# Depthwise convolution of a two-block transformer kernel: 12 of 31 taps as 128x32 weights on TensorE over copies shifted through DRAM, 19 taps on VectorE

## Chip, cores and metric

One core of one Trainium2 chip. The time is the device time of one execution in microseconds, the lower the better. Engines are named as in the profile: PE is TensorE, DVE VectorE, ACT ScalarE, POOL GpSimd, SP SyncE; SP issues almost all DMAs, on one queue.

## Reference

512 tokens, width 1024, fp32. Two blocks follow each other. The first is a mixer (gated linear attention and windowed attention) and an MLP. The second has two layers, `x = x + rms_norm(mixer(rms_norm(x)), post_norm)`: layer 0 mixes with attention and pooling, layer 1 with a gated convolution, which is where most of the change lies:

```python
def odd_mixer(h, w_in, dw_w, dw_b, ln_g, ln_b, w_out):
    proj = h @ w_in                                  # 1024 -> 3072
    a, b, gate = jnp.split(proj, [CONV_WIDTH, 2 * CONV_WIDTH], axis=-1)
    glu = a * jax.nn.sigmoid(b)
    conv = lax.conv_general_dilated(                 # each channel by itself, 31 taps, causal
        glu, dw_w.astype(glu.dtype), window_strides=(1,), padding=[(CONV_K - 1, 0)],
        dimension_numbers=('NWC', 'WIO', 'NWC'), feature_group_count=CONV_WIDTH)
    cf = conv.astype(jnp.float32) + dw_b.astype(jnp.float32)
    mu = jnp.mean(cf, axis=-1, keepdims=True)
    var = jnp.mean(jnp.square(cf - mu), axis=-1, keepdims=True)
    cn = (cf - mu) * lax.rsqrt(var + EPS) * ln_g.astype(jnp.float32) + ln_b.astype(jnp.float32)
    y = jax.nn.silu(cn).astype(h.dtype) * jax.nn.silu(gate)
    return y @ w_out
```

## The kernel before

Everything is written by hand in one program per engine, with semaphores between them; no scheduler moves anything.

**Projections.** Every fp32 weight is split into a high half (ACT, `hi`, L1362) and a low half (DVE, `lo`, L1768); activations are split the same way (`hi_turned` L1403 on ACT, `lo_turned` L1812 on DVE). A product of 128x128 by 128x512 is three matmuls, hi by hi, lo by hi, hi by lo (`mm3`, L702 to L704). A *tile* is one 128x512 result: 8 slices of the contraction by 3, 24 matmuls. Weights come in *chunks* of 512 columns, 2 MB each, loaded by SP (`load_chunk`, L639) in two pieces of four slices into one of two slots, when PE has finished the chunk that was in it two chunks ago. A chunk of the convolution's input projection is four DMAs, since it holds 256 columns of `a` and 256 of `b`; all others are two.

**Convolution stage.** In four chunks (N_AB to N_AB+3) PE makes channel tiles, channels on the partitions and tokens in the row, in pairs: a tile of `b`, to which ACT applies the sigmoid, and a tile of `a` ("gated"), from which DVE makes `glu` of channel tile t = 0 to 7, with 30 zero columns ahead of the tokens. Then come four token tiles of each of the two gate chunks, N_G0 and N_G1, then the output projection, chunks N_CO0 and N_CO1. The 31 taps of channel tile t are spread: 4 are matmuls on PE with diagonal 128x128 weights that ACT builds (`diagonal`, L1628; `conv_taps`, L861, in the middle of the next tile of `b`), 16 are multiply-adds on DVE in two chains in PSUM (`tap`, L2113), 11 are products on ACT (L1644) that POOL adds up (L1291, L1295). DVE adds the sums to `ct` (`conv_sum`, L2123), PE turns it to tokens (`turn_conv`, L850), ACT copies it out (`conv_out`, L1650), and after the last the layernorm follows on DVE (statistics L2129, centred L2161, scaled L2171, product with the gate L2179), PE turning each block of 128 tokens (`turn_block`, L840) for the output projection. The order of DVE and ACT in this stage stands in tables (`hooks`), that of PE in `after`.

**Passages.** Between a projection's last chunk and the next stage stand four blocks of 128 tokens (`boundary_blocks`, s = 0, 1, 2): the square sum of the second half (L1376), the post scale, the new residual on DVE (`rt`, L1795), the pre scale (L1391), `normed` on DVE (`un`, L1804), the turn on PE (L840), the halves of the turned block. Into this both engines fit the weight halves of the following chunk: ACT `hi(following, b - 1)` in blocks 1 and 2, DVE `lo(following, b - 2)` in blocks 2 and 3.

Of the kernel before, what the change touches and what calls it, by code (L numbers as in the profile page):

```python
# [5 lines left out]
F32 = mybir.dt.float32  # L6
# [35 lines left out]
PE_TAPS = 4  # L42
DVE_TAPS = 16
ACT_TAPS = TAPS - DVE_TAPS - PE_TAPS
PRODUCTS = ACT_TAPS + 1
COPY_AT = ACT_TAPS - 2

# [21 lines left out]
def all_tiles():  # L69
# [16 lines left out]
    for n in range(N_AB, N_G0):  # L86
        tiles += [(n, m, m, "AD"[m % 2]) for m in range(4)]
# [21 lines left out]
def chunk_dmas(n):  # L109
    return 2 if N_AB <= n < N_G0 else 1  # L110
# [9 lines left out]

def tap_chain(t, m):

    if m >= DVE_TAPS - 2:
        return 0
    return m % 2 if t < 2 else 1 - m % 2

def tap_order(t):

    return (max(m for m in range(DVE_TAPS) if tap_chain(t, m) == 1) + 1,)

# [24 lines left out]
def shape_constants():  # L157
# [10 lines left out]
                           np.broadcast_to(cnt, (P, 64))], axis=1).astype(np.float32)  # L168
# [41 lines left out]
def block_kernel(nc, a, out):  # L210
    ctx = ExitStack()
    with ctx:
# [22 lines left out]
        act_lo = sb("act_lo", [P, KT, TOK], F32R)  # L235
        R = sb("R", [P, TOK])
# [91 lines left out]
        pacc = at("pacc", [P, 2, TOK], arena + 32 * KB)  # L328
# [7 lines left out]
        diag = at("diag", [P, 2, PE_TAPS, P], arena + 52 * KB)  # L336
# [3 lines left out]
        sg = cC("sg", [P, 2, TOK])  # L340
        prod = cC("prod", [P, 4, TOK])
        ct = cC("ct", [P, 2, TOK])
        taps = cC("taps", [P, KT, TAPS])
        tap_rows = at("tap_rows", [TAPS, D], arena + 84 * KB)
# [17 lines left out]
        def vacc(t, which):  # L362

            return (psT[:, 0, :], psT[:, 1, :], ps6[:, :])[(2 * t + which) % 3]

        relF_dram = nc.dram_tensor("relF_dram", [8, REPEAT, 512], F32, kind="Internal").ap()
# [235 lines left out]
        def _(sp):  # L602
# [96 lines left out]
        def _(pe):  # L699
# [465 lines left out]
            pe.wait_ge(taps_in, 16)  # L1165
            pe.wait_ge(ob_done, 4)
            for k in range(KT):
                last = pe.transpose(ps6[:, k * TAPS:(k + 1) * TAPS], tap_rows[:, k * P:(k + 1) * P],
                                    ident[0:TAPS, 0:TAPS])
            last.then_inc(taps_ps, 1)  # L1170
# [3 lines left out]
            after = {(1, 0): 0, (1, 3): 1, (2, 2): 2, (3, 0): 3, (3, 2): 4}  # L1174
            for i in range(4):
                for m in range(4):
                    channel_tile(N_AB + i, m, 0)
                    if m % 2 == 0 and 2 * i + m // 2 >= 1:
                        conv_taps(2 * i + m // 2 - 1)
                    channel_tile(N_AB + i, m, 1)  # L1180
                    if (i, m) in after:
                        turn_conv(after[i, m])
            after = {(0, 1): 5, (1, 0): 6, (1, 2): 7}
            for i in range(2):
                for b in range(NBLK):
                    token_tile(N_G0 + i, b, 0)
                    if i == 0 and b == 0:
# [18 lines left out]
        def _(pool):  # L1206
# [74 lines left out]
            for slot in range(4):  # L1281
                pool.memset(glu[:, slot, 0:CPAD], 0.0).then_inc(pad_set, 1)
            for t in range(KT):
                for m in range(1, ACT_TAPS + 1):
                    made = PRODUCTS * t + m + 1
                    pool.wait_ge(prod_done, made)
                    g = made - 1
                    if m == 1:
                        if t >= 2:
                            pool.wait_ge(conv_done, t - 1)  # L1290
                        pool.tensor_tensor(pacc[:, t % 2, :], prod[:, (g - 1) % 4, :], prod[:, g % 4, :], ALU.add)\  # L1291
                            .then_inc(padd_done, 1)
                    else:
                        pool.wait_ge(padd_done, ACT_TAPS * t + m - 1)
# [934 lines left out]
```

## Time and profile before

| | |
|---|---|
| median of 3 runs | 1126.48 us (1124.2 to 1126.49) |
| the profiled execution | 1125.93 us, span 1124.1 us |
| mean granted clock of PE | 0.96 |
| PE | 1033.6 us busy, 92% |
| DVE, ACT, POOL | 584.4, 468.5, 170.0 us busy |
| DMA | 93.91 MB, mean 84 GB/s |

In a timeline row, the bracket is the time that the engine stood idle before it and what released it; in a group's row, the idle time stands after the bar.

### The profile page before, as it was taken

To read this page: it belongs to the slowest core of one execution; us is meant where nothing else is said; L and a number is where in the kernel's file an instruction comes from. 1 tells how busy PE (TensorE), PEld (TensorE's weight loads), DVE (VectorE), ACT (ScalarE), POOL (GpSimd) and SP (SyncE) were. 2 spreads that over 40 slices of the span, in tenths; PEclk is the share of its full clock that TensorE was granted. 3 is DMA by queue.
4 is the path that set the end of the run, shared out by engine and by line. 5 is a ranking of instruction groups with operands and counts; after the bars stand their busy time and mean duration, and the time that the engine had idled before them with its cause. 6 is when DMAs were issued, how large, how long until landed. Compare 5 with 4: busy or idle time off the path is not lost.

```text
span 1124.1 us, 12285 instructions
## 1 busy us (share of the span) xinstructions
PE 1033.6 (92%) x4847; PEld 824.7 (73%) x4847; DVE 584.4 (52%) x768; ACT 468.5 (42%) x765; POOL 170.0 (15%) x131
## 2 busy tenths in 40 slices
PE   3899999997999999999999979989898899979897
PEld 2677677886788888888888868767677667657676
DVE  5436665235744234333344463366556397777853
ACT  3325562135533334134123354234355557556541
POOL 2200101000000000000000000022000189886300
PEclk8999999998999999999999999989999799999989
DMA  6532102034221252233224214302033222210301
GB/s 213 73 122 76 38 1 76 1 113 150 76 76 75 75 187 75 75 109 116 76 75 149 76 38 132 141 1 75 2 136 120 68 76 76 75 54 27 145 1 75
DMA packets 55823, 93.91 MB, mean 84 GB/s; under 512 B 2581, under 2 KB 23958, under 8 KB 55638
## 3 DMA queue, kind: packets, MB, share of 16 engines
q1 hardware_dynamic: 53648, 90.61, 23.3%
q10 hardware_dynamic: 2118, 2.52, 1.6%
q8 instruction: 39, 0.64, 0.2%
q14 instruction: 18, 0.15, 0.0%
HBM read 90.76 MB, written 2.36 MB: 83 GB/s over the span
## 4 chain that ended last, share of the span: by engine, by line
PE 55%; DVE 8%; ACT 4%; issue 3%; POOL 1%; DMA 1%; SPq 0%; DVEq 0%; POOLq 0%; ACTq 0%
PE acc L702 17%; PE acc L703 17%; PE acc L704 16%; DVE wlr L1768 2%; ACT wh L1362 2%; DVE psT L2113 1%; POOL pacc L1295 1%; PE psT L861 1%; DMA wl<-in_c_w_in_dram 1%; PE ps L861 1%; PE ps L993 1%; DVE rt L1795 1%; DVE act_lo L1812 1%; ACT junk L1391 1%; PE psT L978 1%
## 5 line engine op out<-in xcount | busy, mean ns | idle before, releaser
L1768 DVE TENSOR_TENSOR wlr<-wl,wh 128x2048 fp32r<-128x2048 f32 (+1 forms) x66 | 149.9, 2276 | 96.4 <-ACT wh L1362 96.4
L702 PE MATMUL acc<-act_hi,wh 128*128 128x512 f32 x464 | 187.9, 405 | 1.7 <-DVE act_lo L1812 1.4
L704 PE MATMUL acc<-act_hi,wlr 128*128 128x512 f32 x464 | 182.3, 393 | 0.0
L703 PE MATMUL acc<-act_lo,wh 128*128 128x512 f32 x464 | 182.1, 392 | 0.0
L1362 ACT ACTIVATE wh<-wl 128x2048 fp32r<-128x2048 f32 (+1 forms) x66 | 123.7, 1880 | 61.2 <-DMA wl<-in_w_up_dram 35.1
L702 PE MATMUL acc<-wh,act_hi 128*128 128x512 f32 x320 | 131.3, 410 | 19.0 <-DVE act_lo L1738 7.6
L703 PE MATMUL acc<-wlr,act_hi 128*128 128x512 f32 x320 | 127.6, 399 | 0.0
L704 PE MATMUL acc<-wh,act_lo 128*128 128x512 f32 x320 | 127.6, 399 | 0.0
L1295 POOL TENSOR_TENSOR pacc<-pacc,prod 128x512 f32<-128x512 f32 x80 | 117.5, 1469 | 28.6 <-ACT prod L1644 16.1
L702 PEld LDWEIGHTS acc<-act_hi,wh 128*128 128x128 f32 x464 | 88.4, 191 | 21.7 <-DVE act_lo L1812 1.8
L703 PEld LDWEIGHTS acc<-act_lo,wh 128*128 128x128 f32 x464 | 88.3, 190 | 19.1 <-issue 1.7
L704 PEld LDWEIGHTS acc<-act_hi,wlr 128*128 128x128 f32 x464 | 87.9, 190 | 19.0
L703 PE MATMUL acc<-wlr,hid_hi 128*128 128x512 f32 x256 | 100.8, 394 | 0.0
L702 PE MATMUL acc<-wh,hid_hi 128*128 128x512 f32 x256 | 100.5, 393 | 0.0
L704 PE MATMUL acc<-wh,hid_lo 128*128 128x512 f32 x256 | 99.4, 388 | 0.0
L702 PEld LDWEIGHTS acc<-wh,act_hi 128*128 128x128 f32 x320 | 61.9, 194 | 34.9 <-DVE act_lo L1738 9.3
L702 PE MATMUL acc<-act_hi,w_hi 128*128 128x512 f32 x152 | 65.5, 431 | 10.8 <-DVE act_lo L1730 7.4
L1276 POOL MEMSET uu<- 128x64 f32 x1 | 0.2, 157 | 475.5 <-PE acc L704 475.5
L703 PEld LDWEIGHTS acc<-wlr,act_hi 128*128 128x128 f32 x320 | 62.3, 195 | 13.0 <-issue 0.7
L704 PEld LDWEIGHTS acc<-wh,act_lo 128*128 128x128 f32 x320 | 61.9, 193 | 13.5
L1644 ACT ACTIVATE prod<-glu,taps 128x512 f32<-128x512 f32 x88 | 60.0, 716 | 13.7 <-POOL pacc L1295 13.0
L2113 DVE SCALAR_TENSOR_TENSOR psT<-glu,taps,psT 128x512 f32<-128x512 f32 x83 | 59.7, 750 | 4.7 <-PE psT L861 4.4
(221 smaller groups left out, 1536.8 us busy)
## 6 DMA issues: line engine op xcount, KB each, us to landing
wl<-in_w_up_dram SPq DMA_DIRECT2D x16, 1024.0 KB, 6.3
wl<-in_w_down_dram SPq DMA_DIRECT2D x16, 1024.0 KB, 6.3
raw<-in_w_in_dram SPq DMA_DIRECT2D x18, 512.0 KB, 4.8
wl<-in_a_w_in_dram SPq DMA_DIRECT2D x8, 1024.0 KB, 6.2
wl<-in_c_w_in_dram SPq DMA_DIRECT2D x16, 512.0 KB, 6.2
wl<-in_w_out_dram SPq DMA_DIRECT2D x4, 1024.0 KB, 6.2
wl<-in_ab_w_out_dram SPq DMA_DIRECT2D x4, 1024.0 KB, 7.4
wl<-in_c_w_in_dram SPq DMA_DIRECT2D x4, 1024.0 KB, 6.4
```

Source lines behind the costliest of these rows:

```text
L702: pe.matmul(dst, hi, x_hi, start=first, stop=False)
L703: pe.matmul(dst, hi, x_lo, start=False, stop=False)
L704: return pe.matmul(dst, lo, x_hi, start=False, stop=last)
L861: last = pe.matmul(vacc(t, 0), diag[:, t % 2, m, :], glu[:, t % 4, j:j + TOK], start=m == 0, stop=m == PE_TAPS - 1)
L978: last = pe.transpose(psTf[:, (2 * b + j) * P:(2 * b + j + 1) * P], LG[layer][:, i % 2, j, 1 + b * P:1 + (b + 1) * P], ident[:, :])
L993: last = pe.matmul(ps6[:, 64 * j:64 * j + 64], PT[layer][:, (2 * b + j) * P:(2 * b + j + 1) * P], VTOK[layer][:, kb, 64 * g:64 * g + 64], ...
L1295: pool.tensor_tensor(pacc[:, t % 2, :], pacc[:, t % 2, :], prod[:, g % 4, :], ALU.add)\
L1362: act.activation(wh[slot][:, kk, cols], wl[slot][:, kk, cols], ACT.Copy).then_inc(whi_done, 1)
L1391: act.activation(junk[:, :], rt[:, b, :], ACT.Square, accum_out=ssq[:, s, 16 + b:17 + b])\
L1644: act.activation(prod[:, g % 4, :], glu[:, t % 4, j:j + TOK], ACT.Copy, scale=taps[:, t, j:j + 1])\
L1768: dve.tensor_tensor(wlr[slot][:, kk, cols], wl[slot][:, kk, cols], wh[slot][:, kk, cols].bitcast(F32), ALU.subtract).then_inc(wlo_done, 1)
L2113: ins = dve.scalar_tensor_tensor(out=sums, in0=src, scalar=taps[:, t, m:m + 1], in1=sums, op0=ALU.mult, op1=ALU.add)
```

## The change

`PE_TAPS` goes from 4 to 12, `ACT_TAPS` to none, DVE has 19 (`Y_TAPS` 10, `X_TAPS` 9).

- **Taps on PE.** SP writes `glu` of channel tile t to DRAM (`glu_dram`, L689) and reads it back four times, 32 channels and all four channel groups at a time, each read one token further (`shifted`, L692). Partitions 32j to 32j+31 then hold the groups of 32 channels shifted by j tokens. For each group of 32 channels (c) three matmuls with 128x32 weights (`tapw`, made by POOL from the taps and a pattern of small identities) sum four taps each, 12 in all, at column position 32c of the array (L884).
- **Taps on DVE.** Ten into a sum in SBUF (`ysum`), nine onto PE's sum in PSUM (`xsum`), those of t between those of t - 1; `conv_sum` adds the two.
- **ACT and POOL** have no part in the sums. POOL makes the low halves of N_CO0.
- **Order.** `conv_taps(t)` stands in the middle of the next gated tile (for tile 7, of the second gate tile), `turn_conv(t)` stands later too; the last turn comes after the last gate tile. The weight halves at passages come one block sooner. In the layernorm block 0 is scaled before block 1 is centred.

```diff
+            def shift(t):
+
+                sp.wait_ge(evD_done, evacs_before(TILE_AT[N_AB, 0], "D") + t + 1)
+                if t >= 2:
+                    sp.wait_ge(petap_done, t - 1)
+                sp.dma_start(glu_dram[t], glu[:, t % 4, :]).then_inc(glu_out, 16)
+                sp.wait_ge(glu_out, 16 * (t + 1))
+                for j in range(4):
+                    sp.dma_start(shifted[32 * j:32 * j + 32, t % 2, :, :],
+                                 bass.AP(glu_dram.tensor, t * P * GLUW + j, [[GLUW, 32], [32 * GLUW, 4], [1, SHIFTED]]))\
+                      .then_inc(shift_in[t % 2], 16)
...
             def conv_taps(t):
 
-                pe.wait_ge(evD_done, evacs_before(TILE_AT[N_AB, 0], "D") + t + 1)
-                pe.wait_ge(diag_done, PE_TAPS * (t + 1))
-                if t >= 2:
-                    pe.wait_ge(conv_done, t - 1)
-                for m in range(PE_TAPS):
-                    j = TAPS - PE_TAPS + m
-                    last = pe.matmul(vacc(t, 0), diag[:, t % 2, m, :], glu[:, t % 4, j:j + TOK],
-                                     start=m == 0, stop=m == PE_TAPS - 1)
+                pe.wait_ge(shift_in[t % 2], 4 * 16 * (t // 2 + 1))
+                pe.wait_ge(tapw_done, t + 1)
+                if t >= 3:
+                    pe.wait_ge(conv_done, t - 2)
+                for m in range(PASSES):
+                    for c in range(4):
+                        last = pe.matmul(xsum(t)[32 * c:32 * c + 32, :], tapw[:, t % 2, 4 * m + c, :],
+                                         shifted[:, t % 2, c, 4 * m:4 * m + TOK], start=m == 0, stop=m == PASSES - 1)
...
-            after = {(1, 0): 0, (1, 3): 1, (2, 2): 2, (3, 0): 3, (3, 2): 4}
+            after = {(1, 2): 0, (2, 1): 1, (2, 3): 2, (3, 1): 3, (3, 3): 4}
...
-                    if m % 2 == 0 and 2 * i + m // 2 >= 1:
+                    if m % 2 == 1 and 2 * i + m // 2 >= 1:
                         conv_taps(2 * i + m // 2 - 1)
...
-            after = {(0, 1): 5, (1, 0): 6, (1, 2): 7}
+            after = {(0, 2): 5, (1, 1): 6, (1, 3): 7}
...
-                    if b in (1, 2):
-                        hi(following, b - 1)
+                    if b == 1 or (b == 0 and s < 2):
+                        hi(following, b)
                     pre_scale(s, b)
+                    if b == 0 and s == 2:
+                        hi(following, 0)
...
-                    if b >= 2:
-                        lo(following, b - 2)
+                    if b in (1, 2):
+                        lo(following, b - 1)
```

The changed order, at three places. **SP's queue in the convolution stage**, before: the chunks N_AB to N_AB+3, with the layernorm's gains between, then N_G0 (`wl`: a weight slot).

```order
L639 DMA wl_136<-in_c_w_in_dram 128x4x256 x4
L639 DMA wl_135<-in_c_w_in_dram 128x4x256 x4
L643 DMA lng<-in_c_ln_g_dram 128x1024
L643 DMA lnb<-in_c_ln_b_dram 128x1024
L639 DMA wl_136<-in_c_w_in_dram 128x4x256 x4
L639 DMA wl_135<-in_c_w_in_dram 128x4x256 x4
L639 DMA wl_136<-in_c_w_in_dram 128x4x512 x2
```

And now, from N_AB to the load of N_AB+3:

```order
L635 DMA wl_138<-in_c_w_in_dram 128x4x256 x4
L635 DMA wl_137<-in_c_w_in_dram 128x4x256 x4
L639 DMA lng<-in_c_ln_g_dram 128x1024
L639 DMA lnb<-in_c_ln_b_dram 128x1024
L689 DMA glu_dram<-glu 128x542
L692 DMA shifted<-glu_dram 32x4x520 x4
L635 DMA wl_138<-in_c_w_in_dram 128x4x256 x4
L689 DMA glu_dram<-glu 128x542
L692 DMA shifted<-glu_dram 32x4x520 x4
L689 DMA glu_dram<-glu 128x542
L692 DMA shifted<-glu_dram 32x4x520 x4
L635 DMA wl_137<-in_c_w_in_dram 128x4x256 x4
```

The load of N_AB+2 stands behind the write and reads of tile 0 and ahead of those of tiles 1 and 2. Behind N_AB+3 follow tiles 3 and 4, N_G0, tiles 5 and 6, N_G1 and tile 7, so the write of every odd tile is issued right behind a chunk.

**PE at the end of the gate tiles**, before: the turn of channel tile 7, and then the last gate tile (24 matmuls) up to the turn of the layernorm's block 0.

```order
L703 MATMUL acc<-wlr_137,act_hi 128x512
L704 MATMUL acc<-wh_139,act_lo 128x512
L850 MATMUL ps<-ident_ones,ct 128x128 x4
L702 MATMUL acc<-wh_139,act_hi 128x512
L703 MATMUL acc<-wlr_137,act_hi 128x512
```

And now:

```order
L725 MATMUL acc<-wh_141,act_hi 128x512
L726 MATMUL acc<-wlr_139,act_hi 128x512
L727 MATMUL acc<-wh_141,act_lo 128x512
L873 MATMUL ps<-ident_ones,ct 128x128 x4
L863 MATMUL psT<-ident_ones,un 128x128 x8
L725 MATMUL acc<-wh_142,act_hi 128x512
```

The turn of `ct` stood 24 matmuls ahead of L840, and now stands right ahead of it (L863).

**DVE in blocks 2 and 3 of the second passage**, before:

```order
L1795 SCALAR_TENSOR_TENSOR rt<-yg,stat,rt 128x1024
L1768 TENSOR_TENSOR wlr_137<-wl_135,wh_139 128x2048
L1812 TENSOR_TENSOR act_lo<-psT,act_hi 128x4x128 x2
L1804 SCALAR_TENSOR_TENSOR un<-rt,stat,gpre 128x1024
L1825 TENSOR_TENSOR yg<-acc,yg 128x512
L1778 TENSOR_TENSOR yg<-yg,gpost 128x512
L1795 SCALAR_TENSOR_TENSOR rt<-yg,stat,rt 128x1024
L1768 TENSOR_TENSOR wlr_137<-wl_135,wh_139 128x2048
L1812 TENSOR_TENSOR act_lo<-psT,act_hi 128x4x128 x2
L1804 SCALAR_TENSOR_TENSOR un<-rt,stat,gpre 128x1024
```

And now:

```order
L1803 SCALAR_TENSOR_TENSOR rt<-yg,stat,rt 128x1024
L1776 TENSOR_TENSOR wlr_139<-wl_137,wh_141 128x2048
L1820 TENSOR_TENSOR act_lo<-psT,act_hi 128x4x128 x2
L1812 SCALAR_TENSOR_TENSOR un<-rt,stat,gpre 128x1024
L1833 TENSOR_TENSOR yg<-acc,yg 128x512
L1786 TENSOR_TENSOR yg<-yg,gpost 128x512
L1803 SCALAR_TENSOR_TENSOR rt<-yg,stat,rt 128x1024
L1820 TENSOR_TENSOR act_lo<-psT,act_hi 128x4x128 x2
L1812 SCALAR_TENSOR_TENSOR un<-rt,stat,gpre 128x1024
```

The low weight half (L1768, now L1776) that stood in block 3, between `rt` and `act_lo`, is gone from there; it stands in block 2, and that of block 2 in block 1.

## Rows read from the trace of the kernel before

**Rows 1.** The page, part 1: busy time, share of the span, instructions of each engine.
```profile
PE 1033.6 (92%) x4847; PEld 824.7 (73%) x4847; DVE 584.4 (52%) x768; ACT 468.5 (42%) x765; POOL 170.0 (15%) x131
```

**Rows 2.** Windows: from:to, length, busy (count) of PE, PEld, DVE, ACT, POOL; PEclk, DMA, GB/s.
```profile
877.70:1056.00 178.30, 166.96 (x654) 122.98 (x655) 128.74 (x165) 108.14 (x165) 127.56 (x88) 0.96 0.18 62
877.80:883.10 5.30, 5.30 (x13) 4.14 (x14) 0.00 (x0) 0.00 (x0) 0.00 (x0) 0.50 0.22 90
957.50:962.90 5.40, 5.38 (x9) 2.33 (x10) 5.36 (x9) 2.04 (x3) 4.83 (x5) 0.68 0.00 0
303.10:306.40 3.30, 3.29 (x8) 2.61 (x9) 2.48 (x3) 0.47 (x1) 0.00 (x0) 0.51 0.37 135
```

**Rows 3.** Waits of PE, 877.7 to 1056: us in total, times, longest.
```profile
PE ps L861 <- DVE ct L2123: 3.8, 1, 3.8
PE psT L861 <- DVE ct L2123: 3.0, 1, 3.0
PE ps L861 <- DVE glu L2093: 3.0, 2, 2.1
PE psT L861 <- DVE glu L2093: 1.4, 1, 1.4
```

**Rows 4.** Timeline of PE, first passage: start, us, line, operation [idle before <- releaser].
```profile
303.11 0.79 PE L702 MATMUL acc<-wh,act_hi 128*128 128x512 f32 x1 [2.37 <-DVE wlr L1768]
```

**Rows 5.** Timeline of PE and DVE, second passage.
```profile
667.49 0.50 PE L702 MATMUL acc<-wh,act_hi 128*128 128x512 f32 x1 [4.40 <-DVE wlr L1768]
...
674.70 1.04 PE L840 MATMUL psT<-ident_ones,un 128*128 128x128 f32 x8
...
668.70 1.28 DVE L1804 SCALAR_TENSOR_TENSOR un<-rt,stat,gpre 128x1024 f32<-128x1024 f32 x1
```

**Rows 6.** Timeline of ACT and PE, third passage.
```profile
853.22 0.60 ACT L1376 ACTIVATE junk<-acc 128x512 f32<-128x512 f32 x1 [0.90 <-PE acc L704]
...
874.41 1.97 PE L840 MATMUL psT<-ident_ones,un 128*128 128x128 f32 x8 [5.64 <-DVE un L1804]
```

**Rows 7.** Timeline of PE: the tap matmuls of the first channel tile.
```profile
894.06 3.60 PE L861 MATMUL psT<-glu,diag 128*128 128x512 f32 x8
```

**Rows 8.** Timeline of PE: matmuls in 64x64 tiles of the array.
```profile
184.19 0.98 PE L1044 MATMUL acc<-va_tok,o 64*64 64x128 f32 x26
...
185.88 0.50 PE L702 MATMUL acc<-act_hi,w_hi 128*128 128x512 f32 x1
```

**Rows 9.** Timeline of PE: one tile of a projection (24 matmuls) and the next.
```profile
899.56 0.39 PE L702 MATMUL acc<-act_hi,wh 128*128 128x512 f32 x1
...
905.00 0.39 PE L702 MATMUL acc<-act_hi,wh 128*128 128x512 f32 x1
```

**Rows 10.** Line L639, weight chunks of c_w_in: issues; us to landing, of three chunks.
```profile
L639 SPq DMA_DIRECT2D wl<-in_c_w_in_dram x4: 378/508/508, 905.9 to 907.4; - x4
...
DMA to landing us min/median/max: 3.5/5.5/8.7
...
DMA to landing us min/median/max: 5.8/6.6/7.5
...
DMA to landing us min/median/max: 5.2/6.8/8.4
```

**Rows 11.** Landing of the `gpost` loads, the `out_dram` stores, the `bias` loads (in this order).
```profile
DMA to landing us min/median/max: 3.9/4.0/8.1
...
DMA to landing us min/median/max: 2.6/2.6/4.6
...
DMA to landing us min/median/max: 3.7/7.4/10.7
```

**Rows 12.** Timeline of DVE and PE, the layernorm's first block.
```profile
1063.42 1.23 DVE L2179 TENSOR_TENSOR un<-un,gate 128x1024 f32<-128x1024 f32 x1 [0.97 <-ACT gate L1612]
...
1064.70 1.97 PE L840 MATMUL psT<-ident_ones,un 128*128 128x128 f32 x8 [4.32 <-DVE un L2179]
```

**Rows 13.** Groups of instructions of POOL: the one 128x2048 subtraction it has.
```profile
L1231 POOL TENSOR_TENSOR w_lo<-raw,w_hi 128x2048 fp32r<-128x2048 f32 x1 | 4.5, 4515 | 18.8 <-ACT w_hi L1327 18.8
```

More of the change, by code:

```diff
@@ L85, in all_tiles @@
         tiles += [(n, b, b, "D") for b in range(NBLK)]
-    for n in range(N_AB, N_G0):
+    for n in range(N_AB, N_AB + 4):
         tiles += [(n, m, m, "AD"[m % 2]) for m in range(4)]
@@ L235, in block_kernel @@
         act_lo = sb("act_lo", [P, KT, TOK], F32R)
+        R_off = top[0]
         R = sb("R", [P, TOK])
@@ L339, in block_kernel @@
         glu = cC("glu", [P, 4, CPAD + TOK])
[L340 to L344, printed above, removed]
+        shifted = cC("shifted", [P, 2, 4, SHIFTED])
+        ct = at("ct", [P, 2, TOK], arena + 48 * KB)
+        tap_rows = at("tap_rows", [TAPS, D], arena + 86 * KB)
+        taps_all = at("taps_all", [P, KT * TAPS + 32 * PASSES], R_off)
+        taps = taps_all[:, 0:KT * TAPS].rearrange("p (k t) -> p k t", k=KT)
+        ptaps = taps_all[:, KT * TAPS:KT * TAPS + 32 * PASSES].rearrange("p (m c) -> p m c", m=PASSES)
+        pattern = at("pattern", [P, 32], R_off + 4 * (KT * TAPS + 32 * PASSES))
+        tapw = at("tapw", [P, 2, 4 * PASSES, 32], sq_off + KB)
+        tap_sets = at("tap_sets", [32 * PASSES, P], sq_off + 5 * KB)
         stat = at("stat", [P, 192], sq_off)
@@ L1282, in _ @@
                 pool.memset(glu[:, slot, 0:CPAD], 0.0).then_inc(pad_set, 1)
+            pool.wait_ge(taps_done, 1)
             for t in range(KT):
[L1284 to L1294, printed above, removed]
-                        pool.tensor_tensor(pacc[:, t % 2, :], pacc[:, t % 2, :], prod[:, g % 4, :], ALU.add)\
-                            .then_inc(padd_done, 1)
+                if t >= 2:
+                    pool.wait_ge(petap_done, t - 1)
+                pool.tensor_tensor(tapw[:, t % 2, :, :].rearrange("p (m c) n -> p m c n", m=PASSES),
+                                   pattern.rearrange("p (m c n) -> p m c n", m=1, c=1).to_broadcast([P, PASSES, 4, 32]),
+                                   ptaps[:, :, 4 * t:4 * t + 4].rearrange("p m (c n) -> p m c n", n=1)
+                                   .to_broadcast([P, PASSES, 4, 32]), ALU.mult).then_inc(tapw_done, 1)
+            for piece in range(2):
+                kk, slot = slice(4 * piece, 4 * piece + 4), N_CO0 % 2
+                pool.wait_ge(whi_done, piece_count(N_CO0, piece))
+                pool.wait_ge(wlo_done, piece_count(N_CO0, piece) - 1)
+                pool.tensor_tensor(wlr[slot][:, kk, :], wl[slot][:, kk, :], wh[slot][:, kk, :].bitcast(F32),
+                                   ALU.subtract).then_inc(wlo_done, 1)
         @block.scalar
@@ L1658, in _ @@
             act.wait_ge(taps_ps, 1)
[L1659 to L1661 removed]
+            act.activation(taps_all[:, :], ps6[:, 0:KT * TAPS + 32 * PASSES], ACT.Copy).then_inc(taps_done, 1)
             sigmoid(0)
@@ L2090, in gated @@
                 if t >= 4:
[L2091 to L2092 removed]
+                    dve.wait_ge(shift_in[t % 2], 4 * 16 * (t // 2 - 1))
+                    dve.wait_ge(x_step, X_TAPS * (t - 3))
                 dve.tensor_tensor(glu[:, t % 4, CPAD:], acc[:, TILES[e][2], :], sg[:, t % 2, :], ALU.mult)\
                    .then_inc(evD_done, 1)
[L2096 to L2115 removed]
@@ new lines, in y_tap @@
+            def y_tap(t, i):
+                src, sums = glu[:, t % 4, PE_TAPS + i:PE_TAPS + i + TOK], ysum[:, t % 2, :]
+                scale = taps[:, t, PE_TAPS + i:PE_TAPS + i + 1]
+                if i == 0:
+                    dve.wait_ge(evD_done, evacs_before(TILE_AT[N_AB, 0], "D") + t + 1)
+                    if t >= 2:
+                        dve.wait_ge(conv_done, t - 1)
+                    ins = dve.tensor_scalar(sums, src, scale, vec[:, V_DWB + t:V_DWB + t + 1], ALU.mult, ALU.add)
+                else:
+                    dve.wait_ge(y_step, Y_TAPS * t + i)
+                    ins = dve.scalar_tensor_tensor(out=sums, in0=src, scalar=scale, in1=sums, op0=ALU.mult, op1=ALU.add)
+                ins.then_inc(y_step, 1)
@@ L2117, in conv_sum, with x_tap @@
+            def x_tap(t, i):
+                j = PE_TAPS + Y_TAPS + i
+                if i == 0:
+                    dve.wait_ge(petap_done, t + 1)
+                else:
+                    dve.wait_ge(x_step, X_TAPS * t + i)
+                dve.scalar_tensor_tensor(out=xsum(t), in0=glu[:, t % 4, j:j + TOK], scalar=taps[:, t, j:j + 1],
+                                         in1=xsum(t), op0=ALU.mult, op1=ALU.add).then_inc(x_step, 1)
             def conv_sum(t):
-                dve.wait_ge(padd_done, ACT_TAPS * (t + 1))
```

216 lines of the change are left out of this document (98 added, 118 removed).

## Prediction

> **What bounds the kernel now.** The page comes first: TensorE (PE) is busy for 92% of the span, no other engine for more than 52% [rows 1]. So a microsecond counts only if it shortens or lengthens what PE does or waits for. The windows view, cut to the stage of the convolution, says how much that is: from 877.70 to 1056.00 PE is busy 166.96 of 178.30 us, while DVE has 128.74, ACT 108.14 and POOL 127.56 [rows 2]. The view of waits of that stage names what is left: 3.8, 3.0, 3.0 and 1.4 us, all in front of the tap matmuls of L861 (for a `ct` or a `glu` that DVE was late with) [rows 3]. The timeline at the three passages shows where PE stands for weight halves or for `un` [rows 4 to 6]. The same windows carry the clock. After a wait PE runs at the lower of its two levels for a while: PEclk 0.50 in 877.80 to 883.10, behind a wait of 5.64 us, 0.68 in 957.50 to 962.90, behind one of 2.1 [rows 2, 3, 6]. A long wait therefore costs itself and then some 2.6 us more (half of 5.3).
>
> All sums are made against the profiled execution, 1125.93 us with a span of 1124.1. It lies inside the three runs shown (1124.2 to 1126.49, median 1126.48), 0.5 us under their median.
>
> **Passages.** At s=0 PE waits 2.37 us for the second low half [rows 4], which is now made a block sooner, before the turn that PE also needs; the 3.3 us behind it at clock 0.51 [rows 2] cost 1.7. Both go: **-4.1**. At s=1 PE stands 4.40 us up to 667.49 for the same kind of half, does 24 matmuls, and turns block 3 at 674.70 [rows 5]. Without the wait the 24 (5.4 us, [rows 9]) are over at 668.5, and block 3 is turned when DVE's `un` of it ends, 668.70 + 1.28 [rows 5]. DVE's list is only reordered, its total up to that `un` is the same, so the turn comes at 670.05: **-4.65**. At s=2 PE waits 5.64 us for `un` of block 3 [rows 6], the end of a chain through ACT and DVE. The diff puts a high half (1.9 us, L1362) behind block 0's scale, in front of block 1's square, where ACT had 0.90 us to spare [rows 6]: the chain starts 1.0 later. The low half that leaves DVE in block 3 lay beside it. **+1.0**. Together **-7.8**.
>
> **Tap matmuls.** Before: four of 128x512 in 3.45 us, eight times ([rows 7]; the row's 3.60 runs to the modelled end of the last, which lies beside the next matmul, and I count 0.15 for that), so 0.86 each, 27.6. After: twelve of 32 columns per channel tile, four at a time in the array's four column groups. The nearest row is L1044, where 28 matmuls of 64x64 tiles that lie in different quarters run from 184.19 to 185.88, 1.69 us [rows 8]: 0.060 each where one alone would need 0.215 (a quarter of 0.86 for 128 columns), 3.56 times faster. Twelve then take 12 x 0.86 / 3.56 = 2.9 us. The bounds are 2.6 (four at once) and 10.3 (one at a time). I take 2.9: 23.2 against 27.6, **-4.4**. The Trainium skill's page "TensorE: Matmul & The Clock Gate" (Part 3) gives 2.38 times for three column tiles and says that a weight load overlaps matmuls in flight only where the row group differs, which column tiles do not do; by 2.38 of 3 the eight groups would cost 3 us more than I take. No row of this case has column tiles alone.
>
> **Old waits** of L861 go with what made them: **-11.2** [rows 3]. DVE gets 24 more taps of the kind it has (at its mean of 0.78 us an instruction [rows 2], +19) and gives up two low halves (2.3 each): about 143 of 178, no bound. ACT loses 88 products, POOL 88 sums. What POOL gets, eight `tapw` of 128x384 and two low halves of 4.5 us [rows 13], lies beside PE's last token tiles. I price them at nothing; if the second half came late, the first matmul of the output projection would wait, up to 4.5.
>
> **New waits.** The taps of tile t now need glu(t) in DRAM and back. SP does that in order, on one queue. Counted from T, the end of the `gated` PE tile: glu is made by T + 0.9; the conv_taps stand half a pair later, 1.5 PE tiles of 5.44 us [rows 9], at T + 8.2. The write (277 KB) takes 2.2, from 2.6 us for 512 KB of the same direction, `out_dram` [rows 11]. The four reads (266 KB each, 1.06 MB in all) take 5.6: 1 MB of weights lands 5.2 us after its issue [rows 10], and I add 0.4 for four issues in place of one. Below stands 4.0, the single 512 KB of `gpost` [rows 11]; above 8.1, from the eight `bias` loads of 192 KB onto 16 partitions each: issued 0.45 us apart, they land 3.7 (the first) to 10.7 us (the last) after their issue, so (10.7 + 7 x 0.45 - 3.7) / 7 = 1.45 us apart, and the fourth (768 KB) 8.1 after the first issue [rows 11]. I take 5.6, since pieces of 2,080 bytes are nearest to the weights' 2,048. With 0.4 for SP in all the data is there at T + 9.1 (0.9 + 2.2 + 5.6 + 0.4), so a free queue costs **1.0** a tile: even t, four times, 4.0. Odd t: glu(t) ends with a weight chunk, and SP issues the next 2 MB load ahead of shift(t). Does the write queue behind it? `gpost`, 512 KB, lands 8.1 us after its issue behind a chunk and 4.0 alone [rows 11]: it does. The last piece of a chunk lands 8.7, 7.5 and 8.4 us after its own issue [rows 10], and that issue is 1.5 us after the first where there are four pieces, 0.4 where there are two. I take the middle, 8.1, and 0.6 for the write's own packets behind it (an estimate: 1.0 at the 3.6 us of a second MB, less because the latency has been paid). So the write lands at T + 0.1 + 1.5 + 8.1 + 0.6 = T + 10.3, the reads, with 0.3 for SP, at T + 16.2, wait **8.0** (t = 1, 3); with two pieces it is T + 15.1, wait **6.9** (t = 5, 7). Sum of the eight: 4.0 + 16.0 + 13.8 = **+33.8**. Queued behind them on PE is the rest of the same tile, so nothing hides them.
>
> **Clock.** Four long waits, 2.65 each, +10.6; the three stretches at 0.68 that follow today's waits of 2 to 3.8 us go, 5.4 x 0.35 or 1.9 each [rows 2], -5.7. **+4.9**.
>
> **The last tile.** turn_conv(7) stood ahead of the last gate tile, whose 5.4 us ran inside the chain to the layernorm, where PE ended waiting 4.32 us for `un` [rows 12]. It now stands behind that tile: **+5.4**. The chain itself gets shorter: the low half leaves DVE (0.8 of it on the path), block 0 is scaled before block 1 is centred, and a gate goes ahead, for which the product waited 0.97 [rows 12]: **-2.4**.
>
> The four small loads of tap sets and pattern go ahead of the mixer's first weight chunks, tapw needs them first for tile 0: nothing.
>
> **Sum:** -7.8 - 4.4 - 11.2 + 33.8 + 4.9 + 5.4 - 2.4 = +18.3, so **1144.2 us**.
>
> **Rivals.** A, *the queue is shared, not waited for* (faster). If the write's packets slip between those of the chunk, odd tiles wait as even ones. All terms but new waits and their clock make -26.1; the kernel becomes faster when waits and clock stay under 26.1, that is when an odd tile waits less than about 3.8 us (4 x 1.0 + 4 x 3.8 + 4 x 1.7 = 26.0). At 1.0 to 2.5 each it gives 1108 to 1121, say 1115. `gpost` speaks against it; for it, that no row shows a write to DRAM behind a chunk. Chance 0.19.
> B, *column tiles don't run side by side*. Two at once: 5.2 instead of 2.9, +18, 1162. One at a time: 10.3, +59, 1203. L1044 speaks against, but its tiles differ in rows too. 0.09.
> C, *the reads crawl*, since each touches 32 partitions. By the `bias` row 8.1 instead of 5.6, 2.5 x 8 = +20, 1164. For it: `bias` moved some 130 KB a microsecond on 16 partitions, while the second 1 MB of a chunk lands 0.4 + 8.4 - 5.2 = 3.6 us after the first, some 290 KB a microsecond [rows 10, 11]. 0.20. The Trainium skill ("SBUF — State Buffer", Door 1: The DMA port swizzle) says that 32 partitions reach only 8 of the 16 ports, 218 GB/s; an estimate by that page is 4.9 us of moving for 1.06 MB instead of 3.7, +1.2 a trip, +10, 1154.
> My forecast has 0.52.
>
> **How the numbers follow.** 1144 is the likeliest case. 0.2% (2.3 us) is about what a measurement of this kernel tells from no change. The faster side is A, 0.19; 0.03 for within 0.2% is the lower tail of the forecast (odd waits near 4); the rest, 0.78, is slower. The range goes from A's upper part, 1118, over the short read (4.0 instead of 5.6, eight times: 1131) to C's 1164 with three over; outside lie the lower half of A and most of B.
>
> **What would show it.** Right: PE waits at the tap line (L884) named after the shifted loads, four of 6 to 8 us at odd t, four near 1; a group of twelve in 2.6 to 3.0 us; PEclk 0.5 behind the long waits; no wait for low halves at the first two passages; turn_conv(7) as PE's last work before the layernorm. Wrong: odd waits no longer than even ones (A), a group of 5 or 10 us (B), the four reads landed only 8 us after their first issue (C), or a wait at the output projection for a half from POOL.

## The result, and the profile after

| | before | changed |
|---|---|---|
| median (range) | 1125.34 us (1124.13 to 1126.49), 4 runs | 1148.86 us (1146.78 to 1151.21), 4 runs |
| ratio | | 1.021, 95% interval 1.0185 to 1.0234 |
| profiled execution, span | 1125.93, 1124.1 us | 1146.78, 1145.0 us |

The change makes the kernel 23.5 us slower by the medians, 20.9 by the two spans. The prediction said 1144.2, 18.3 over the profiled execution, with 1118 to 1167 as its range. The spans are what is taken apart here; the changed kernel's profiled execution is its fastest of the four, and what the other 2 to 4 us of the others are is not in a trace.

The page of the changed kernel, part 1, answers to [rows 1]:

```profile
PE 1029.3 (90%) x4976; PEld 814.9 (71%) x4976; DVE 594.3 (52%) x790; ACT 398.4 (35%) x637; POOL 61.1 (5%) x53
```

PE has less to do than before (1029.3 against 1033.6) and still ends later; POOL's 170.0 have become 61.1, ACT's 468.5 are 398.4. So the time is in waits and in the clock. Windows of the convolution stage and of five stretches behind waits, with the columns of [rows 2]:

```profile
868.40:1077.60 209.20, 170.41 (x797) 119.05 (x798) 138.85 (x187) 38.22 (x37) 18.44 (x10) 0.90 0.37 104
914.60:922.00 7.40, 7.36 (x38) 3.64 (x39) 0.19 (x1) 0.00 (x0) 0.83 (x1) 0.80 0.00 0
954.10:962.00 7.90, 7.90 (x38) 3.46 (x39) 0.00 (x0) 0.00 (x0) 0.83 (x1) 0.72 0.00 0
994.00:1002.00 8.00, 7.96 (x35) 3.22 (x36) 0.00 (x0) 0.00 (x0) 0.83 (x1) 0.66 0.01 2
1013.00:1022.00 9.00, 9.00 (x46) 4.86 (x47) 7.79 (x12) 1.07 (x2) 0.00 (x0) 0.81 0.05 5
1036.00:1045.00 9.00, 8.74 (x41) 4.30 (x42) 5.53 (x7) 0.93 (x2) 0.00 (x0) 0.76 0.00 0
```

The first row runs from the stage's first matmul to the turn of channel tile 7: PE busy for 170.41 of 209.20 us. The timeline of PE in that stage, all eight groups of tap matmuls (x24 counts two records for each of the twelve), answers to [rows 3] and [rows 7]:

```profile
868.51 0.80 PE L725 MATMUL acc<-act_hi,wh 128*128 128x512 f32 x1 [1.41 <-DVE act_lo L1820]
...
891.81 2.78 PE L884 MATMUL psT<-shifted,tapw 128*32 128x512 f32 x24 [1.82 <-DMA shifted<-glu_dram]
...
914.64 4.19 PE L884 MATMUL psT<-shifted,tapw 128*32 128x512 f32 x24 [8.96 <-DMA shifted<-glu_dram]
...
931.64 2.79 PE L884 MATMUL ps<-shifted,tapw 128*32 128x512 f32 x24 [1.22 <-DMA shifted<-glu_dram]
...
954.09 4.93 PE L884 MATMUL psT<-shifted,tapw 128*32 128x512 f32 x24 [8.56 <-DMA shifted<-glu_dram]
...
972.49 2.78 PE L884 MATMUL psT<-shifted,tapw 128*32 128x512 f32 x24 [1.83 <-DMA shifted<-glu_dram]
...
994.04 5.35 PE L884 MATMUL ps<-shifted,tapw 128*32 128x512 f32 x24 [7.18 <-DMA shifted<-glu_dram]
...
1013.00 4.48 PE L884 MATMUL psT<-shifted,tapw 128*32 128x512 f32 x24 [1.95 <-DMA shifted<-glu_dram]
...
1036.26 4.82 PE L884 MATMUL psT<-shifted,tapw 128*32 128x512 f32 x24 [7.18 <-DMA shifted<-glu_dram]
```

The waits are 1.82, 8.96, 1.22, 8.56, 1.83, 7.18, 1.95 and 7.18: 38.7 us where the old kernel's were 11.2. A long one at every odd t, a short one at every even t. At full clock a group takes 2.78 us. SP's queue around the first long wait, and the landing of the eight writes:

```profile
897.55 2.04 SPq L635 DMA_DIRECT2D wl<-in_c_w_in_dram  x4
899.64 0.66 SPq L689 DMA_DIRECT2D glu_dram<-glu  x1
907.75 1.75 SPq L692 DMA_DIRECT2D shifted<-glu_dram  x4
```

```profile
DMA to landing us min/median/max: 2.2/4.8/8.1
```

The chunk goes out at 897.55, the write of tile 1 behind it at 899.64, and SP can issue the reads only at 907.75, when the write has landed: 8.1 us after its issue, the longest of the eight; the shortest took 2.2. The chunk's last piece, issued at 899.1, landed 7.9 us later, at 907.0, so the write landed behind it. The taps start 6.9 us after the reads' first issue, at 914.64. The end of the stage:

```profile
1077.52 0.60 PE L873 MATMUL ps<-ident_ones,ct 128*128 128x128 f32 x4
...
1085.69 1.97 PE L863 MATMUL psT<-ident_ones,un 128*128 128x128 f32 x8 [7.57 <-DVE un L2191]
...
1090.44 0.80 PE L725 MATMUL acc<-wh,act_hi 128*128 128x512 f32 x1 [2.77 <-DVE act_lo L1820]
```

### The profile page after: what moved, and what is told of

Same layout as the page of the kernel before. It is cut to its first block, busy times and chain, and to the rows that moved or that the text cites. A ratio compares the mean times of both kernels' runs of the same rounds, so it can differ in the third digit from the quotient of the medians.

```text
span 1145.0 us, 12308 instructions
## 1 busy us (share of the span) xinstructions
PE 1029.3 (90%) x4976; PEld 814.9 (71%) x4976; DVE 594.3 (52%) x790; ACT 398.4 (35%) x637; POOL 61.1 (5%) x53
## 4 chain that ended last, share of the span: by engine, by line
PE 66%; DVE 9%; DMA 6%; ACT 4%; issue 3%; SPq 1%; DVEq 0%
PE acc L725 18%; PE acc L726 18%; PE acc L727 18%; DMA glu_dram<-glu 3%; DMA shifted<-glu_dram 3%; PE psT L884 2%; PE ps L1016 1%; ACT wh L1385 1%; DVE wlr L1776 1%; PE psT L1102 1%; PE psT L1001 1%; DVE ysum L2115 1%; PE acc L990 1%; DVE psT L2125 1%; PE psT L863 1%
## 5 line engine op out<-in xcount | busy, mean ns | idle before, releaser
L1776 DVE TENSOR_TENSOR wlr<-wl,wh 128x2048 fp32r<-128x2048 f32 (+1 forms) x64 | 144.1, 2256 | 91.2 <-ACT wh L1385 91.2
L727 PE MATMUL acc<-act_hi,w_lo 128*128 128x512 f32 x152 | 61.6, 405 | 0.0
L726 PE MATMUL acc<-act_lo,w_hi 128*128 128x512 f32 x152 | 61.6, 405 | 0.0
L725 PEld LDWEIGHTS acc<-wh,hid_hi 128*128 128x128 f32 x256 | 48.1, 188 | 11.1
L727 PEld LDWEIGHTS acc<-wh,hid_lo 128*128 128x128 f32 x256 | 48.1, 188 | 10.7
```

Of the source, the lines that this page charges most:

```text
L725: pe.matmul(dst, hi, x_hi, start=first, stop=False)
L726: pe.matmul(dst, hi, x_lo, start=False, stop=False)
L727: return pe.matmul(dst, lo, x_hi, start=False, stop=last)
L1776: dve.tensor_tensor(wlr[slot][:, kk, cols], wl[slot][:, kk, cols], wh[slot][:, kk, cols].bitcast(F32), ALU.subtract).then_inc(wlo_done, 1)
```

## The experiments

Ten kernels were run, each timed against the kernel before on the same chip (its medians there: 1126.44 for the first four, 1124.90 for the next four, 1126.14 for the last two). "The change" is the changed kernel.

### The shift ahead of the chunk

```diff
-            load_chunk(N_AB + 2, c_in, ((0, 512, CW), (CW, D + 512, CW)))
             shift(1)
+            load_chunk(N_AB + 2, c_in, ((0, 512, CW), (CW, D + 512, CW)))
             shift(2)
...
```

(and so for tiles 3, 5 and 7)

> Each odd channel tile's write and reads are issued ahead of the weight chunk that frees at the same moment, all else as in the change. Theory (the queue is first in, first out, and the write of an odd tile stands behind 2 MB): the four long waits of PE (9.0, 8.6, 7.2, 7.2 us) fall to about 1.8, the write lands 2.2 to 3 us after its issue; the chunk now starts some 5 us later and ends as the next even tile's write is issued, so the even waits at t = 2 and 4 rise from 1.2 to 1.8 to as much as 4. Sum of the eight waits about 18 instead of 38.7, half-clock stretches some 5 us cheaper: about 1124 us (1120 to 1130). Rival (the transfer is slow because PE, DVE and DMA are busy at that moment, not because of its place in the queue): odd waits stay above 5 us, 1140 or more.

Measured: 1121.62 us, ratio 0.9961 (0.9947 to 0.9975): 27 us less than the change, and faster than the kernel before. SP's queue at the same place, and PE's waits for shifted data in the stage:

```profile
897.84 0.34 SPq L689 DMA_DIRECT2D glu_dram<-glu  x1
899.97 1.73 SPq L692 DMA_DIRECT2D shifted<-glu_dram  x4
901.75 2.08 SPq L635 DMA_DIRECT2D wl<-in_c_w_in_dram  x4
```

```profile
PE psT L884 <- DMA shifted<-glu_dram: 15.0, 6, 3.9
PE ps L884 <- DMA shifted<-glu_dram: 4.4, 2, 2.6
```

The write lands in 2.1 us and the reads follow; the eight waits sum to 19.4 (expected 18). The chunk, started 4 us later, is still there in time. What made the long waits is the 2 MB that the write was issued behind, and not how busy the engines are at that moment. The longest of the eight, 3.9, is at tile 3, and some 2 us of it (an estimate) are DVE's: it starts that `glu` at 930.80, where the gated tile ends at about 928.7, because a low weight half of 2.3 us stands in its list ahead. In the change the same `glu` starts at 939.88, 2.5 us after PE has freed the chunk's slot (937.41), and the chunk hides it.

### A queue of its own for the shift

```diff
-                sp.dma_start(glu_dram[t], glu[:, t % 4, :]).then_inc(glu_out, 16)
-                sp.wait_ge(glu_out, 16 * (t + 1))
+                act.dma_start(glu_dram[t], glu[:, t % 4, :]).then_inc(glu_out, 16)
+                act.wait_ge(glu_out, 16 * (t + 1))
...
             sigmoid(1)
+            shift(1)
             sigmoid(2)
+            shift(2)
```

(all of `shift`, and all eight calls; SP issues weight chunks alone)

> The writes and reads are issued by ScalarE on its own queue, the weight chunks stay on SyncE's; so a write never stands behind a chunk in a queue, but moves beside it through the same 16 engines. Theory (order in the queue makes the wait): the write of an odd tile lands 2.5 to 4 us after its issue instead of 6.7 to 8.1, its reads take longer since they share with the chunk (8 to 9 us instead of 7.0), odd waits 3 to 5 us, time about 1130. Rival (the engines work off everything in the order of issue, whatever the queue): odd waits stay at 7 to 9, time as the change's 1148.

Measured: 1145.32 us, ratio 1.0169 (1.0145 to 1.0192). PE's waits for shifted data, and the landing of the writes:

```profile
PE psT L864 <- DMA shifted<-glu_dram: 26.7, 6, 9.7
PE ps L864 <- DMA shifted<-glu_dram: 8.0, 2, 6.8
```

```profile
DMA to landing us min/median/max: 2.1/2.8/7.6
```

A window over the write of tile 1, with the columns of [rows 2], and the landing of the chunk's last two pieces, issued at 899.5 and 900.1:

```profile
899.30:904.70 5.40, 5.40 (x26) 4.46 (x25) 5.40 (x9) 0.00 (x0) 0.00 (x0) 1.00 0.95 297
```

```profile
DMA to landing us min/median/max: 6.6/7.2/7.9
```

34.7 us of waits against 38.7. Neither expectation holds. The write of tile 1 is issued at 899.26 and lands at 904.70, ahead of the chunk's last pieces (about 907), so packets of two queues do mix. It still takes 5.4 us where 2.1 is the shortest, with the DMA engines busy for 95% of that time. The longest write, of tile 3, takes 7.6 us; the wait of 9.7 is behind it, and 2.6 us of the delay are again DVE's late `glu` (938.39, the chunk issued from 935.7), which here nothing hides. So a queue of its own takes 4 us off the waits, and standing ahead of the chunk takes 19. "The write queues behind the chunk" was right for one queue and in what it costs, and only part of why the trip is slow at that place.

### The last turn ahead of the last gate tile

```diff
-            after = {(0, 2): 5, (1, 1): 6, (1, 3): 7}
+            after = {(0, 2): 5, (1, 1): 6, (1, 2): 7}
```

> turn_conv(7) stands ahead of the last gate tile again, all else as in the change. Theory (the last gate tile of 5.4 us was taken out of the layernorm's shadow): ct(7) is there in time (made at 1070.0, the place is at 1072.1), PE's wait before the first turned block falls from 7.6 to about 2.1, the time by 5.0 to 5.5 us, to about 1143.5. Rival (the layernorm chain waits for the last gate, not for the turn): under 2 us gained.

Measured: 1144.51 us, ratio 1.0159 (1.0132 to 1.0187); one execution of the four, of 2604.94 us, is in the median but not in the ratio (the median of the other three is 1142.35). By the ratios that is 0.005, some 6 us, under the change, with intervals that touch. In the trace:

```profile
1080.56 1.61 PE L863 MATMUL psT<-ident_ones,un 128*128 128x128 f32 x8 [3.56 <-DVE un L2191]
```

The wait has fallen from 7.57 to 3.56 and not to 2.1. The turn comes 5.4 us sooner as against the last tile, but ACT serves the second-last gate and a table load ahead of copying the turned tile out, which takes 1.4 back. Neither expectation holds exactly; it is near the first. The last tile had been taken out of the layernorm's shadow, as predicted; the step was worth 4.0 there instead of 5.4.

### Wide reads, two ways

First four reads of all 128 partitions each, with the four shifts as the outermost dimension:

```diff
-                for j in range(4):
-                    sp.dma_start(shifted[32 * j:32 * j + 32, t % 2, :, :],
-                                 bass.AP(glu_dram.tensor, t * P * GLUW + j, [[GLUW, 32], [32 * GLUW, 4], [1, SHIFTED]]))\
+                for c in range(4):
+                    sp.dma_start(shifted[:, t % 2, c, :],
+                                 bass.AP(glu_dram.tensor, (t * P + 32 * c) * GLUW, [[1, 4], [GLUW, 32], [1, SHIFTED]]))\
```

> The same bytes are read in four DMAs that each write all 128 partitions (one group of 32 channels in its four shifts) instead of 32 partitions each, all else as in the change. Theory (a read onto 32 partitions is slow because of the few partitions): the last read lands some 5.6 us after the first issue instead of 7.0, each of the eight waits is 1.4 us shorter, and with fewer half-clock stretches the time falls by 11 to 14 us, to about 1136. Rival (the reads cost what their packets of 2,080 bytes and the fixed part of a DMA cost): landing and time stay within 0.3 us and 3 us of the change's.

Measured: 1204.75 us, ratio 1.0715 (1.0686 to 1.0745), 56 us more than the change, and neither expectation. PE's waits:

```profile
PE psT L884 <- DMA shifted<-glu_dram: 70.8, 6, 16.5
PE ps L884 <- DMA shifted<-glu_dram: 21.4, 2, 13.6
```

The DMA view of this kernel over tile 0's reads (883 to 897 us, 40 slices: busy share in tenths of the 16 engines, then GB/s, then packets, MB and share):

```profile
DMA  0000011222222222222222222222222222222000
GB/s 0 0 0 0 0 18 36 113 95 101 83 107 89 65 95 101 89 101 95 95 89 107 107 95 95 113 101 95 107 101 101 95 107 107 95 101 107 36 0 0
q1 hardware_dynamic: 528, 1.07, 20.6%
```

And of the change over its own reads of tile 0 (884 to 893 us):

```profile
DMA  5000000593799999989999999999531000000000
GB/s 212 0 0 0 0 0 0 65 157 83 250 342 342 296 268 213 203 176 213 222 213 287 240 194 231 194 176 185 102 56 28 0 0 0 0 0 0 0 0 0
q1 hardware_dynamic: 614, 1.11, 55.8%
```

The same megabyte moves at about 100 GB/s with two tenths of the engines busy, against mostly 180 to 340 with nearly all. That fits four of the sixteen engines at work, as many as the outermost dimension has entries. The next run tests whether the outermost dimension does it: the channels outermost, `[[GLUW, 32], [1, 4], [1, SHIFTED]]`, so partition 4q+j holds channel q shifted by j; the pattern and the tap weights are permuted to match by one small copy on POOL.

> The same bytes again in four reads of 128 partitions, but with the 32 channels as the outermost dimension of each read (partition 4q+j holds channel q shifted by j; the tap weights are permuted to match) where e3_wide_reads had the 4 shifts outermost. Theory (e3_wide_reads was slow because its outermost dimension of 4 put each read on 4 of the 16 engines, and 128 partitions as such are no harm): all 16 engines move it, the waits fall from 93 us in sum back to 39 or less. If few partitions also slow the change's reads, as forecast's rival C had it, the last read lands 5.6 us after the first issue instead of 7.0 and the time is about 1137; if not, 1147 to 1150, as the change. Rival (writes to 128 partitions out of overlapping rows are slow in themselves): waits stay above 80 us, 1200.

Measured: 1138.09 us, ratio 1.0127 (1.0098 to 1.0156), as expected for both halves of the theory: 11 us under the change. The first three even tiles in its timeline (L886 is its tap line; the middle row is cut off by the end of its window), and the landing of its 32 reads; of the change's below it:

```profile
894.91 2.79 PE L886 MATMUL psT<-shifted,tapw 128*32 128x512 f32 x24 [0.62 <-DMA shifted<-glu_dram]
...
934.20 1.07 PE L886 MATMUL ps<-shifted,tapw 128*32 128x512 f32 x8 [0.50 <-DMA shifted<-glu_dram]
...
974.70 2.79 PE L886 MATMUL psT<-shifted,tapw 128*32 128x512 f32 x24 [0.46 <-DMA shifted<-glu_dram]
```

```profile
DMA to landing us min/median/max: 2.9/3.5/4.3
```

```profile
DMA to landing us min/median/max: 3.2/4.6/5.8
```

The last of four reads lands at most 4.3 us after its issue instead of 5.8, and the even waits are 0.5 to 0.9 instead of 1.2 to 1.95. All eight sum to 32.2. From the reads' first issue to the taps it is 6.0 us on average where the change has 7.0, though SP needs 0.7 us longer to issue the four. So a read onto 32 partitions was slow, by some 1.0 us a trip; the packets are as long as before and the outermost dimension is 32 in both. The trace is of the slowest of the four executions (1144.28 us), in which the stage begins 4.3 us later than in the change's. From the stage's first matmul to the output projection's it has 215.1 us against 221.9, so 6.8 of the 11 us are seen, 6.5 of them waits, and the rest is not. That exactly four engines worked in e3_wide_reads is not shown by itself; that its outermost dimension of 4 made it slow is.

### The passages alone

On the kernel before:

```diff
-                    if b in (1, 2):
-                        hi(following, b - 1)
+                    if b == 1 or (b == 0 and s < 2):
+                        hi(following, b)
                     pre_scale(s, b)
+                    if b == 0 and s == 2:
+                        hi(following, 0)
...
-                    if b >= 2:
-                        lo(following, b - 2)
+                    if b in (1, 2):
+                        lo(following, b - 1)
```

> Only the two edits at the passages (weight halves one block sooner), on the kernel before; the convolution is as it was. Theory (the two parts of the change add up): the first matmul of the convolution stage comes some 9.3 us sooner, as in the change's profile (868.5 against 877.8), nothing later changes, and the time is about 1117 us, 0.8% below the kernel before. Rival (the shift is eaten by the convolution stage, where PE then waits for what DVE and SP bring no sooner): less than 5 us gained.

Measured: 1115.97 us, ratio 0.9919 (0.9904 to 0.9934). The stage's first matmul:

```profile
867.96 0.79 PE L702 MATMUL acc<-act_hi,wh 128*128 128x512 f32 x1 [1.41 <-DVE act_lo L1814]
```

It starts at 867.96 where it started at 877.79, and the stage behind it waits as before (3.8, 3.3, 2.9 and 1.4). The parts add up: the passages give 9, the convolution takes 30 to 32.

### Both orders mended

The diffs of e1_shift_first and e2_turn7_early together.

> The edits of e1_shift_first and e2_turn7_early together. Both theories hold independently: 1121.6 minus 4.4, about 1117 us (1114 to 1119). Rival (with the shorter waits ct(7) comes too late for the early turn, so PE waits there instead): 1120 or more.

Measured: 1119.91 us (1115.18 to 1124.12, ten runs), ratio 0.9952 (0.9935 to 0.9969), 2 us under the first alone. That is 0.9 above the expected range and not the rival either: PE waits for no `ct`. Its waits for shifted data sum to 18.8, the wait at the layernorm is 3.6. From the stage's first matmul to the output projection's it has 194.1 us where e1_shift_first has 197.0. The waits are 4.6 less, and most of the 1.7 between is the clock: three tap groups are slow (4.3 to 5.4 us) where two were. The stage also begins 1.7 us later in this execution. A wait of 3.31 us was followed by a group at half clock and one of 2.54 was not, nor one of 2.63 in e1_shift_first; that this is what moves the time from execution to execution is likely but not shown.

### The taps half a tile later

```diff
-                    if m % 2 == 1 and 2 * i + m // 2 >= 1:
-                        conv_taps(2 * i + m // 2 - 1)
                     channel_tile(N_AB + i, m, 1)
+                    if m % 2 == 1 and 2 * i + m // 2 >= 1:
+                        conv_taps(2 * i + m // 2 - 1)
```

(and the same for tile 7 in the second gate tile), first with both orders mended:

> As e7_first_and_turn7, and conv_taps(t) stands after the second half of the gated tile instead of between its halves, 2.7 us later. Theory (the trip through DRAM needs about 10 us from the gated tile's end, and only what exceeds the place of the taps is paid): seven of the eight waits, 1.7 to 2.6 us, vanish, those behind a late chunk (3.9, 3.5) shrink to about 1; some 17 us of waits become 2 to 4, and one half-clock stretch goes: about 1100 to 1103 us. Rival (DVE, which starts its nine taps on PE's sum only after conv_taps, then becomes late with ct and PE waits at the turns): 1110 or more.

Measured: 1094.66 us, ratio 0.9742 (0.9716 to 0.9768). All waits of PE in the stage and up to the output projection:

```profile
PE psT L863 <- DVE un L1812: 5.6, 1, 5.6
PE acc L725 <- DVE act_lo L1820: 4.7, 2, 3.3
PE psT L863 <- DVE un L2191: 3.6, 1, 3.6
PE psT L884 <- DMA shifted<-glu_dram: 0.7, 1, 0.7
```

0.7 us is left of the waits for shifted data, at tile 3, where DVE's `glu` is late. Then the same edit on the change, with nothing else:

> The change with conv_taps(t) 2.7 us later and nothing else: SP's order, reads and turns are the change's. Theory (each wait is what the trip exceeds the place of the taps by): the four short waits (1.2 to 1.95) go, the four long ones shrink by 2.7 each, from 32.0 to 21 in sum, so 17.5 us of wait less, and the half-clock stretches behind long waits stay: about 1130 us (1127 to 1134). Rival (once a write stands behind a chunk, nothing short of another order helps, because the later place of the taps also delays the next gated tile and with it the next write): under 10 us gained.

Measured: 1111.04 us, ratio 0.9871 (0.9849 to 0.9892): 38 us under the change where some 19 were expected. Tile 1, tile 2 (an even one, without a wait), and tiles 5 and 7:

```profile
910.13 4.48 PE L884 MATMUL psT<-shifted,tapw 128*32 128x512 f32 x24 [3.70 <-DMA shifted<-glu_dram]
...
926.13 2.79 PE L884 MATMUL ps<-shifted,tapw 128*32 128x512 f32 x24
...
973.39 2.79 PE L884 MATMUL ps<-shifted,tapw 128*32 128x512 f32 x24 [1.60 <-DMA shifted<-glu_dram]
...
1003.39 2.79 PE L884 MATMUL psT<-shifted,tapw 128*32 128x512 f32 x24 [1.51 <-DMA shifted<-glu_dram]
```

The waits sum to 10.0. The expectation had the place of the taps wrong: conv_taps(t-1) stood ahead of the gated tile's end, from which the trip of t is counted, and now stands behind it. With its own 2.8 us between, the taps of t come 2.7 + 2.8 = 5.5 later as seen from the write, and four long waits lose 4 x 5.5 = 22 (31.9 to 10.0); the four short ones, 6.8 in all, are gone. The clock gives most of the rest: of these groups only tile 1's is slow, where five of eight were.

Last, e8_taps_half_later with the reads of e6_wide_many_rows, as a candidate:

> e8_taps_half_later with the reads of e6_wide_many_rows. Theory (PE pays only what of the trip sticks out behind the place of the taps): e8_taps_half_later has 0.7 us of waits for shifted data left, so a read that lands some 2 us sooner gives at most that, 1094 us, within 0.2% of e8_taps_half_later. Rival (the shorter reads also free the DMA engines for the weight chunks, for whose halves something waits): 1092 or less.

Measured: 1094.81 us, ratio 0.9718 (0.9703 to 0.9733), the same as without them. Reads that are hidden are worth nothing when they get faster. The two are the best kernels of the study, 2.6 to 2.8% under the kernel before.

## Why the prediction came out right

Sign, size and mechanism held; the forecast of 18.3 met 20.9 in the trace. The terms as measured below, -9.3 - 5.4 - 11.2 + 38.7 + 5.1 + 3.2, make 21.1. That the sum came so near is in part luck: the read was put too short at every tile, 10.9 us in all, and the errors that offset it were not foreseen. By its steps:

- **Passages**, -7.8: measured -9.3 (the stage's first matmul at 868.51 instead of 877.79). The first passage gave 4.0 (4.1), the third cost 0.8 (1.0). In the second the last turn came after 23.5 us from the first instead of 28.2, the 4.65 of the sum, and 1.4 more had gone by the third passage's first turn; that was not in the sum.
- **Tap matmuls**, -4.4: 8 x 2.78 = 22.2 at full clock against 27.6, -5.4. Four column tiles run 12 x 0.86 / 2.78 = 3.7 times as fast as one after another, so rival B falls. The Trainium skill's rule ("TensorE: Matmul & The Clock Gate", Part 3) that a weight load overlaps only where row groups differ, with 2.38 for three tiles, would have given 3.3 us a group (an estimate by that page); these rows do not show such a cost.
- **Old waits**, -11.2: gone. No wait for `ct` or `glu` is left in the stage.
- **New waits**, +33.8: 38.7. The step "the write stands behind the chunk" met its number: the forecast had the write of tile 1 land 10.3 us after the gated tile's end, and the trace has it 10.2 us after the chunk's issue, which follows that end (907.75 - 897.55). What was too small is the read: taken as 5.6, it was 6.8 to 7.1 us from the first issue to the taps, 10.9 more in all. Of that 3.8 was offset because the reads were issued sooner than the sum had them: at even tiles 2.9, 2.9, 3.5 and 3.6 us after the gated tile's end (taken as the start of `glu`) instead of 3.5, at odd ones 10.2, 9.9, 8.7 and 8.8 (after the chunk's issue) instead of 10.6, 10.6, 9.5 and 9.5. Another 2.3 was offset because a turn stands ahead of the taps at five of the eight tiles, 0.45 us each, which the sum did not have. What stays is 2.8 at the four even tiles (6.8 instead of 4.0) and 2.1 at the odd ones (31.9 instead of 29.8). The longer read was rival C in small: the few partitions a read touches. The Trainium skill ("SBUF — State Buffer", Door 1: The DMA port swizzle) states that 32 partitions reach half the ports; the 1.2 us a trip estimated by it in the prediction is near the 1.1 that e6_wide_many_rows took off the even waits (0.55 off the odd ones). C's own price, 8.1 from the `bias` rows, was too high.
- **Clock**, +4.9: the five stretches in the windows cost 7.4 x 0.20 + 7.9 x 0.28 + 8.0 x 0.34 + 9.0 x 0.19 + 9.0 x 0.24 = 10.3, against 5.2 for the old ones: +5.1. The prediction had 5.7 there, since it took 0.35 for what PEclk 0.68 leaves (0.32; the three windows have 0.68, 0.69 and 0.68). The forecast had four new stretches of 2.65; there are five of 1.5 to 2.7, the fifth behind a wait of only 1.95.
- **Last tile**, +5.4, and **layernorm chain**, -2.4: PE's wait before the first turned block grew from 4.32 to 7.57, +3.2 where the two terms make +3.0. From the turn of tile 7 to the output projection's first matmul the trace has 12.9 us where it had 15.2, and the old stretch holds the last gate tile, 5.4 us of work, which PE now does before it. Moving the turn back was worth 4.0 of the 5.4.
- **Nothing for POOL and DVE**: DVE is busy 138.85 of 209 us, and POOL's second low half ends at 1073.9, 16 us before its matmul. Inside the stage DVE is not quite free: it is 2.5 us late with the `glu` of tile 3, which costs nothing behind a chunk and shows in e1_shift_first.
- **Range**: its 1131 for a short read takes off 1.6 eight times, but an even tile had only 1.0 of wait to lose, so it should be 1134. Nothing hangs on it.

Rival A, *the queue is shared*, falls as it was put: an odd tile does not wait as an even one. But e4_act_queue shows that its picture of packets that mix is true of two queues, and that it helps little: mixed with 2 MB, the write still lands after up to 7.6 us.

## What to carry to other kernels

A round trip through DRAM costs what of it sticks out behind the place where its result is used; moving that place by 5.5 us took 28.7 us of waits away and 38 us in all, since what PE waits it pays again in clock. A small urgent transfer must be issued ahead of the large one that is released at the same moment, and a second queue did not replace that here. Before a redesign is judged, count where its waits come from: this one was 2.1% slower in the order given and 2.6% faster in another.

## What the runs showed of the hardware

- Four reads whose access pattern has an outermost dimension of 4 moved 1.06 MB at about 100 GB/s with two tenths of the DMA engines' time in use, and took 13.3 us from the first issue to the taps (tile 0); with 32 outermost, the same bytes to the same 128 partitions took 5.7 to 6.2 us.
- A write of 277 KB issued behind 2 MB on one queue landed behind it (907.75 against 907.0); on a second queue it landed ahead of the 2 MB's last pieces (904.70 against about 907), after 5.4 us instead of 2.1 to 2.4 alone.
- Twelve fp32 matmuls of 128x32 weights over 512 columns took 2.78 us in four column groups, weight loads included.
- Whether PE's clock falls behind a wait is not a matter of its length alone: waits of 1.82 and 1.22 us left the group at 2.78 us, one of 1.95 was followed by a group of 4.48. In e10_later_alone a wait of 3.23 left it at 2.79, in e7_first_and_turn7 one of 3.31 was followed by 5.35.
